# Mixture-of-experts weight stream: the down weights are loaded one expert later, and the first two gate-and-up products run back to back

## The reference

```python
def expert_block(args):
    xblk, e = args
    h = jax.nn.silu(xblk @ w_gate[e]) * (xblk @ w_up[e])
    return h @ w_down[e]
...
yb = lax.map(expert_block, (xb, block_expert)).reshape(n_rows, d)
return jnp.zeros_like(x2).at[tok_buf].add(yb * gate_buf[:, None])
```

## Time and profile before

| | |
|---|---|
| Median of 3 runs | 1589.25 us (1589.19 to 1590.61) |
| Profiled execution: its time / its span | 1589.6 us / 1587.9 us |
| Expert phase of layer 0 (DMA issue at its start to the last row scatter) | 243.4 to 743.7 us |
| Expert phase of layer 1 (the same) | 1083.2 us to the end |
| PE busy over the span | 1421.8 us (90%) |
| Weights and rows read from HBM over the span | 458.44 MB, written 12.58 MB |
| DMA in the middle of both expert phases | 420 to 422 GB/s in nearly every slice |

### The profile page before, as it was taken

How to read it: one execution, slowest core, us unless ns; L and a number is a source line. 1 busy time by engine, 2 the same in 40 slices (tenths; PEclk the granted TensorE clock), 3 DMA queues, 4 the chain that set the end, 5 groups by cost and what they waited for, 6 DMA issues and landing times. The chain is left out here.

```text
span 1587.9 us, 16020 instructions
## 1 busy us (share of the span) xinstructions
PE 1421.8 (90%) x6550; PEld 789.7 (50%) x6550; DVE 501.1 (32%) x1028; ACT 282.2 (18%) x483; POOL 52.8 (3%) x66
## 2 busy tenths in 40 slices
PE   6999866999999899998799986784999998999996
PEld 5878663444433343435487875572443443333432
DVE  2355662122121121221544238654121221221221
ACT  3231420010110110111443213330010110110111
POOL 0000100000000000000000000010000000000000
PEclk9999977999999999999999997786999999999998
DMA  8520557899999999996132020547899999999992
GB/s 242 185 80 0 203 224 271 354 421 421 420 420 422 421 421 420 422 420 247 54 106 92 15 107 0 199 161 270 354 420 421 421 421 421 421 422 420 421 421 99
DMA packets 96532, 463.72 MB, mean 292 GB/s; under 512 B 10952, under 2 KB 31432, under 8 KB 47304
## 3 DMA queue, kind: packets, MB, share of 16 engines
q1 hardware_dynamic: 91848, 454.26, 71.0%
q0 software_dynamic: 4608, 8.40, 1.4%
HBM read 458.44 MB, written 12.58 MB: 297 GB/s over the span
## 5 line engine op out<-in xcount | busy, mean ns | idle before, releaser
L985 PE MATMUL bank<-ring,xT 128*64 128x512 f32 x2048 | 464.1, 606 | 35.0 <-DMA ring<-in_w_up 33.3
L985 PEld LDWEIGHTS bank<-ring,xT 128*64 128x64 f32 x2048 | 144.5, 139 | 308.1 <-issue 264.9
L1025 PE MATMUL bank<-ring,hidT 128*64 128x512 f32 x1024 | 234.3, 599 | 1.1 <-issue 1.1
L1204 DVE COPY xT<-bank 128x512 f32<-128x512 f32 x64 | 44.3, 692 | 536.2 <-PE bank L967 536.2
L967 PEld LDWEIGHTS bank<-x_sb 128*128 128x128 f32 x512 | 124.2, 328 | 72.1 <-issue 48.7
L967 PE MATMUL bank<-x_sb 128*128 128x128 f32 x512 | 136.2, 412 | 23.3 <-DMA x_sb<-x_rows,tok_of_slot 23.3
L1025 PEld LDWEIGHTS bank<-ring,hidT 128*64 128x64 f32 x1024 | 67.8, 137 | 157.0 <-issue 156.8
L1128 ACT ACTIVATE hid<-bank 128x256 f32<-128x256 f32 x64 | 24.5, 383 | 494.0 <-PE bank L985 494.0
L1134 ACT COPY y<-bank 128x512 f32<-128x512 f32 x64 | 37.5, 586 | 384.0 <-PE bank L1025 384.0
L1214 DVE COPY hidT<-bank 128x256 f32<-128x256 f32 x64 | 27.1, 423 | 180.1 <-PE bank L999 180.1
L1042 PE MATMUL bank<-y,x_sb 64*128 64x512 f32 x256 | 72.3, 641 | 2.2 <-ACT y L1134 1.4
(11 more groups left out here) (270 smaller groups left out, 1437.2 us busy)
## 6 DMA issues: line engine op xcount, KB each, us to landing
ring<-in_w_down SPq DMA_DIRECT2D x62, 2048.0 KB, 20.3
ring<-in_w_gate SPq DMA_DIRECT2D x60, 2048.0 KB, 20.8
ring<-in_w_up SPq DMA_DIRECT2D x60, 2048.0 KB, 29.3
ring<-in_mlstm_w_in SPq DMA_DIRECT2D x6, 2048.0 KB, 7.8
ring<-in_conv_w_in SPq DMA_DIRECT2D x18, 512.0 KB, 6.5
ring<-in_w_out SPq DMA_DIRECT2D x2, 4096.0 KB, 14.3
ring<-in_w_gate SPq DMA_DIRECT2D x8, 1024.0 KB, 17.1
ring<-in_w_up SPq DMA_DIRECT2D x8, 1024.0 KB, 27.1
```

Source lines behind the costliest of these rows:

```text
L985: last = nc.tensor.matmul(GU_BANK[e % 2][64 * f:64 * f + 64, :], xgT[e // 2 % 2][:, 4 * h + c, 64 * (e % 2):64 * (e % 2) + 64], gu[:, :, h ...
L1025: last = nc.tensor.matmul(Y_BANK[e % 2][64 * n:64 * n + 64, :], hidT[e % 2][:, c, 64 * f:64 * f + 64], dn[:, f, c, 512 * n:512 * n + 512], ...
L1204: V.tensor_copy(xgT[q % 2][:, 4 * h:4 * h + 4, :], o[:, :].rearrange("p (c r) -> p c r", c=4)).then_inc(xcopied, 1)
```

## The change

In SP's stream, down of expert `e - 1` is now issued behind gate and up of expert `e`, instead of down of expert `e` there; its wait is on the same slot as before, and the stream's last part is in the order gate and up 30, down 29, gate and up 31, down 30, down 31. In PE's program `gate_up(1)` follows directly on `gate_up(0)`; the turning of rows for expert 2, `code_gates` and `turn_hidden(0)` come after it, and the down product of expert 0 after these. At the end the two halves of `gate_up(30)` stand together ahead of `combine(28)` and `down(29)`, and `turn_hidden(30)` ahead of `gate_up(31)`. The work, the bytes and the number of instructions are the same.

```diff
                         for e in range(3, LAST - 1):
                             sp.wait_ge(gu_done, e - 2)
                             load_gate_up(sp, l, e, e % 3, in_gu[l][e % 3])
-                            sp.wait_ge(y_done, e - 2)
-                            load_down(sp, l, e, e % 3, in_dn[l][e % 3])
+                            if e > 3:
+                                sp.wait_ge(y_done, e - 3)
+                                load_down(sp, l, e - 1, (e - 1) % 3, in_dn[l][(e - 1) % 3])
...
-                            sp.wait_ge(y_done, e - 2)
-                            if r == 0:
-                                load_down(sp, l, e, r, in_dn[l][r])
+                            sp.wait_ge(y_done, e - 3)
+                            load_down(sp, l, e - 1, (e - 1) % 3, in_dn[l][(e - 1) % 3])
+                        sp.wait_ge(y_done, LAST - 2)
                         for f in range(2):
...
                         for e in range(LAST - 1):
                             gate_up(e)
+                            if e == 0:
+                                continue
+                            if e == 1:
+                                turn_rows(2)
+                                code_gates()
+                                turn_hidden(0)
                             turn_rows(e + 2)
-                            if e == 0:
-                                code_gates()
                             if e >= 2:
                                 combine(e - 2)
...
                         gate_up(LAST - 1, halves=(0,))
+                        gate_up(LAST - 1, halves=(1,))
                         combine(LAST - 3)
                         down(LAST - 2)
-                        gate_up(LAST - 1, halves=(1,))
+                        turn_hidden(LAST - 1)
                         gate_up(LAST, halves=(0,))
-                        turn_hidden(LAST - 1)
                         gate_up(LAST, halves=(1,))
```

## The result

The changed kernel takes 1569.05 us (median of 4 runs, 1566.72 to 1569.55) against 1589.22 for the kernel before, a ratio of 0.986 with a 95% interval of 0.9842 to 0.9878. Run again later it took 1569.37 us, ratio 0.9868 (0.9849 to 0.9888). 20 us, or 1.3 to 1.4%, are won. The profiled execution took 1568.99 us, its span is 1567.3. The new lines shift the numbers by five or less: gate and up products are now line 986, down 1026, row turning 968, the transposes of `mem` 1097.

The account below looks back on a forecast made before the run. The weight stream, through the landing of `up` of expert 31, was taken to bound the expert phase. Layer 1's 10.6 us plus layer 0's 9.7 make 20.3, giving 1569.0 us; range 1563 to 1578.

Parts of the forecast that it names:

- The bound: Expert phase: landing of `up` of expert 31 ends it; reordering PE's side buys nothing by itself.
- The hole: Stream start: SP's wait for `down(0)` leaves engines idle; closing it wins 5.9 us (bounds 5.3, 6.4) layer 1, 6.5 layer 0.
- The hole closes, with about 1 us to spare: Layer 1 stream start: next release at 1131.05, when 10 MB issued so far have, by the mean engine, until 1133.
- the third release: End of `gate_up(2)` in layer 1, expected at 1131.05 us, with a thin margin of about 1 us.
- What stands ahead of the last gate and up: Stream end: down of expert 30 goes behind gate and up of expert 31, 2 MB less ahead, 5.0 us in each layer.
- in two places only: Reordering the stream pays only at the hole at the start and at what stands ahead of the last gate and up.
- Down of expert 30: End of layer 1: lands 5.0 us after `up` of expert 31, PE wants it 4.64 after; wait of 0.3 us.
- `mem`: After layer 0's experts: lands 6.5 us earlier, at 726.4, PE at 725.0; with 3.2 us of slack, layer 0 wins 9.7.
- Layer 1: Layer 1's gain: 10.9 us earlier landing of `up` of expert 31 minus a 0.3 us wait, 10.6 us.
- Edits at nothing: Moved PE pieces take as long as before; `down(0)` loses cover, its operand just covered; else some tenths later, queue holding 7 us.
- First wait at expert 22, about 6 us of waits: Layer 1, changed kernel: PE's first wait for `up` at about expert 22 instead of 14, about 6 us in all.
- rival 3: Middle of phase: late down weights, excess over 10.2 us paid by every one of 29 experts, two layers; 1615 at 11; chance 0.07.

Follow-up runs that it names:

- the kernel with only the start: Against the kernel before: PE's start changed, its end as before; SP takes down one expert later up to expert 20, then the old order; 1578.3 us, ratio 0.9928.

## Why the prediction was right, and where it was not

Predicted 1569.0, measured 1569.05. That it agrees to a tenth is luck; by its steps:

- *The bound.* Right. PE's order alone buys nothing, the stream's alone buys all of it.
- *The hole* (5.9 and 6.5 us). Right in kind: the rate, the landings 9.9 us apart, and the 11.0 us of the kernel with only the start. That kernel's trace gives 5.7 and 6.0 us: the term was 0.2 and 0.5 too large. "The hole closes, with about 1 us to spare" was not quite so: the third release came 1.4 us later than reckoned, behind the slower `down(0)`, and some 0.8 us of data are missing there. The Trainium skill names specific DMA engines as one thing that a DMA-bound kernel can be bound on (Perfetto Trace Analysis, What "DMA-bound" means). Layer 1's 5.7 lies nearer to the bound from the slowest engines' landings (5.3) than to the other (6.4), which agrees; but in layer 0 the landings gave 6.5 for a measured 6.0, so these runs do not decide between the two bounds.
- *What stands ahead of the last gate and up* (5.0 us). 4.7 and 4.8 were measured. The size is right for the whole change, the reason was too narrow. I wrote that reordering pays "in two places only" and put this one at the last expert. Moving only that load gave 1.1 us of 8, not clear of nothing; beginning seven experts earlier gave 8 to 9. I had written in the next paragraph that PE is nearly late itself, and had not drawn the conclusion.
- *Down of expert 30*, 0.3 us: 0.21 and 0.19.
- *`mem`*: expected at 726.4 with a wait of 1.4 us, came at 727.3 with 1.27. PE reached it at 726.06, 1 us later than expected. Layer 0 gave 8.15 instead of 9.7: 8.8 at `mem` and at the copy behind it, and 0.7 was lost in the transposes at its end, where one group took 1.93 us instead of 1.16.
- *Layer 1* gave 12.4 instead of 10.6. The 2.3 us ahead of the stream are not the change's doing as far as the runs show: over the thirteen profiles the distance from the phase's first DMA to `up` of expert 3 was 21.9 to 22.5 us in ten and 24.0 to 24.4 in three (the kernel before, PE's part alone and down two experts later), and both of PE's starts are in both groups. The first products begin at the low clock there (PE's clock is 0.50 up to 1100 in the kernel before), and how soon it rises differs from run to run. So one miss of +2 and one of -1.5 cancelled.
- *Edits at nothing.* Wrong for `down(0)`: it costs 1.4 to 1.7 us more through the clock. It did little harm, for the reason given there (a queue with data in it), but its 1.4 us used up the 1 us to spare at the third release. SP's part alone, where it is not slow, takes the same time. The operand itself was in time.
- *First wait at expert 22, about 6 us of waits*: expert 22, and 8.7 us.
- *Rivals.* A hole that stays open was seen when the old order came back at expert 4 (1589). The price of rival 3 was wrong, as the kernel with down two experts later showed: a late operand in a stream that keeps its pace is paid once, not in every expert. By that, an estimate from the prediction's own figures, the change would have turned slower not from 10.6 us but from about 20 (10 us of excess in each of two layers).

## What to carry to other kernels

Issue prefetches in the order of use, and give each load its own release: a load that waits behind another's longer wait in one queue leaves a hole of its own, and taking only the first one earlier moves the hole. Where a stream and an engine run at nearly the same pace, an earlier landing is worth no more than the engine can catch up before the end, so count how many steps are left. And price a late operand once for each stream, not once for each use, as long as the stream itself is not held back; one kernel here shows that.

## What was not expected of the hardware

- Row gathers and scatters, 4.2 MB in a layer, cost the weight stream 0.6 us an expert (15.5 instead of 14.9 with 3.1 MB of them left out), and with them about half of the DMA engines are done some 10 us ahead of the others at the end (share 0.56 to 0.48 from 1535 to 1545 us).
- A DMA issue on SP takes 0.4 to 0.5 us early in a phase, where at most 8 MB issued before it have not landed. In the changed kernel each of the 36 issues from 1350 to 1515 us takes 2.1 to 7.5 us, with 8 to 12 MB not landed; the DMA engines stay at 421 GB/s meanwhile, so it cost nothing there. Behind the experts of layer 0 the issue of `mem` took 10.85 us with 7 MB not landed, and 13.14 us with SP's part alone.
- A down product behind some 5 us of small products and transposes ran at a granted clock of 0.68 to 0.72 and took 5.05 to 5.35 us instead of 3.65, in both layers of all eight profiles with that order and in none of the five with the old one.
